# Memory attention in a two-block transformer kernel: GpSimd takes the low parts of the output projection's weights, and two orders of work change

## The reference, cut to what matters

```python
def _memory_cross_attention(h, mem, norm_mem_kv, w_q_mem, w_kv_mem, w_o_mem):
    B, S, _ = h.shape                                    # 1, 256, 1024
    q = (h @ w_q_mem).reshape(B, S, MEM_HEADS, MEM_HEAD_DIM)      # 4 heads of 128
    kv = _rmsnorm(mem, norm_mem_kv) @ w_kv_mem
    k, v = jnp.split(kv, 2, axis=-1)
    ...
    logits = jnp.einsum('bshd,bmhd->bhsm', q, k).astype(jnp.float32) * MEM_HEAD_DIM ** -0.5
    p = jax.nn.softmax(logits, axis=-1).astype(v.dtype)
    o = jnp.einsum('bhsm,bmhd->bshd', p, v).reshape(B, S, MEM_WIDTH)
    return o @ w_o_mem

        # in first_block:
        x = x + _rmsnorm(_memory_cross_attention(h, mem, ...), norm_mem_post)
        h = _rmsnorm(x, norm_ffn_pre)
        x = x + _rmsnorm(_swiglu(h, w_gate_up, w_down), norm_ffn_post)
```

## Time and profile before

| | |
|---|---|
| median of 3 runs | 1464.11 us (1464.03 to 1464.86) |
| the profiled execution's own time | 1464.0 us |
| its span, first to last instruction | 1462.2 us |
| busy share of the span: TensorE, VectorE, ScalarE, GpSimd | 99%, 74%, 47%, 14% |
| mean granted TensorE clock | 0.998 of full speed |
| the memory attention's heads and output projection | 218 to 246 us of the span |
| the norm, to the second block's transposes | 246 to 255 us |

### The profile page before, as it was taken

The page is one execution under the profiler, slowest core; times in us unless marked ns, Lnnn a source line. Parts: engine busy times, 40 slices in busy tenths (PEclk is TensorE's granted clock), DMA queues, the critical chain, the costliest instruction groups (busy, mean ns, idle before and its releaser), DMA issues.

```text
span 1462.2 us, 20856 instructions
## 1 busy us (share of the span) xinstructions
PE 1443.1 (99%) x7488; PEld 1219.0 (83%) x7488; DVE 1088.5 (74%) x1825; ACT 688.2 (47%) x854; POOL 207.4 (14%) x189
## 2 busy tenths in 40 slices
PE   9999999999999999999999999999999999999997
PEld 8988897888888888889988888888888897788886
DVE  5665767888778877757758877777887777688876
ACT  5346556444444444454435443465444377444442
POOL 1073011200001000300032000301000335510001
PEclk9999999999999999999999999999999999999999
DMA  8754653855656556566567566576556450475561
GB/s 275 243 173 142 198 174 124 299 188 182 212 183 213 172 188 213 172 207 198 169 206 237 172 198 206 174 239 212 179 180 217 144 183 30 132 239 176 179 214 66
DMA packets 198876, 274.48 MB, mean 188 GB/s; under 512 B 9632, under 2 KB 158240, under 8 KB 198560
## 3 DMA queue, kind: packets, MB, share of 16 engines
q1 hardware_dynamic: 194304, 256.62, 53.2%
q0 software_dynamic: 4368, 16.78, 3.3%
q10 hardware_dynamic: 144, 0.26, 0.0%
HBM read 272.32 MB, written 1.31 MB: 187 GB/s over the span
## 4 chain that ended last, share of the span: by engine, by line
PE 89%; DVE 3%; POOL 3%; ACT 3%; issue 1%; DMA 0%; DVEq 0%; SPq 0%; ACTq 0%; POOLq 0%
PE ps L646 25%; PE ps L647 25%; PE ps L648 25%; PE ps L758 3%; PE ps L752 3%; PE ps L741 3%; PE ps L687 1%; ACT whi L1415 1%; POOL wlo L2764 1%; DVE wlo L1986 1%; PE ps L805 1%; PE ps L1126 0%; PE ps L1254 0%; DVE big L2588 0%; POOL big L2809 0%
## 5 line engine op out<-in xcount | busy, mean ns | idle before, releaser
L1986 DVE TENSOR_TENSOR wlo<-raw,whi 128x2048 fp32r<-128x2048 f32 (+1 forms) x224 | 509.4, 2291 | 168.4 <-ACT whi L1415 166.5
L1415 ACT CAST whi<-raw 128x2048 fp32r<-128x2048 f32 (+1 forms) x239 | 452.7, 1894 | 373.0 <-PE ps L648 327.8
L646 PE MATMUL ps<-whi,st_hi 128*128 128x512 f32 (+1 forms) x1064 | 414.8, 390 | 0.3 <-DVE wlo L1986 0.3
L648 PE MATMUL ps<-whi,st_lo 128*128 128x512 f32 (+1 forms) x1064 | 412.5, 388 | 0.0
L647 PE MATMUL ps<-wlo,st_hi 128*128 128x512 f32 (+1 forms) x1064 | 412.4, 388 | 0.0
L2400 DVE STREAM_TRANSPOSE hidT<-hidden 32x128 f32<-32x128 f32 x800 | 242.3, 303 | 12.3
L646 PEld LDWEIGHTS ps<-whi,st_hi 128*128 128x128 f32 (+1 forms) x1064 | 198.9, 187 | 41.6 <-DVE wlo L1986 0.6
L648 PEld LDWEIGHTS ps<-whi,st_lo 128*128 128x128 f32 (+1 forms) x1064 | 198.8, 187 | 41.0
L647 PEld LDWEIGHTS ps<-wlo,st_hi 128*128 128x128 f32 (+1 forms) x1064 | 198.9, 187 | 40.0
L646 PE MATMUL ps<-whi,hid_hi 128*128 128x512 f32 x400 | 156.2, 390 | 0.0
L648 PE MATMUL ps<-whi,hid_lo 128*128 128x512 f32 x400 | 155.7, 389 | 0.0
(11 more groups left out here) (261 smaller groups left out, 1430.0 us busy)
## 6 DMA issues: line engine op xcount, KB each, us to landing
raw<-in_ffn_w SPq DMA_DIRECT2D x264, 512.0 KB, 4.8
raw<-in_w_gate_up SPq DMA_DIRECT2D x44, 512.0 KB, 4.7
raw<-in_w_in SPq DMA_DIRECT2D x32, 512.0 KB, 5.1
raw<-in_sgu_w_in SPq DMA_DIRECT2D x32, 512.0 KB, 4.7
raw<-in_w_down SPq DMA_DIRECT2D x22, 512.0 KB, 5.1
raw<-in_sgu_w_out SPq DMA_DIRECT2D x16, 512.0 KB, 4.7
raw<-in_kv_w SPq DMA_DIRECT2D x12, 512.0 KB, 4.5
raw<-in_w_proj_attn SPq DMA_DIRECT2D x8, 512.0 KB, 4.5
```

What stands on the lines that cost most here:

```text
L646: pe.matmul(o, a[0], b[0], start=start, stop=False)
L648: return pe.matmul(o, a[1], b[0], start=False, stop=stop)
L1415: act.copy(whi[:, s, 0:n], raw[:, s, 0:n]).then_inc(whi_ready, 1)
L1986: dve.tensor_tensor(wlo[:, s, 0:n], raw[:, s, 0:n], whi[:, s, 0:n].bitcast(F32), ALU.subtract).then_inc(wlo_ready, 1)
```

## The change

GpSimd's set gets om0 and om1, and GpSimd's program splits both right behind the load of the gain of the FFN's norm, ahead of the roots of the output. VectorE's calls at these two places go. ScalarE casts om1 right behind om0, before the exponentials. In the norm, VectorE scales both halves of block 1 before it brings block 0's first transposed part out, then adds block 1's two halves to the residual, and only then brings out block 0's second part.

```diff
-        BY_POOL |= {first["ffn", n] + 3 for n in range(5)}
+        BY_POOL |= {first["ffn", n] + 3 for n in range(5)} | {first["om"], first["om"] + 1}
...
             queries_out_m(0)
             beside(first["qm"])
+            beside(first["qm"] + 1)
             exp_m(0)
             exp_m(1)
             queries_out_m(1)
             turned_m(0)
-            beside(first["qm"] + 1)
             turned_m(1)
...
-            beside(first["qm"])
             max_m(0)
             max_m(1)
...
             heads_low_m(0)
             heads_low_m(1)
-            beside(first["qm"] + 1)
             heads_low_m(2)
             heads_low_m(3)
...
             scale_rms("mem", "ymem", 1, 0)
-            st_out("ffn0", 0)
             scale_rms("mem", "ymem", 1, 1)
+            st_out("ffn0", 0, part=0)
             add_rms("mem", "ymem", 1)
+            st_out("ffn0", 0, part=1)
             split_half(last + 2, 1)
...
             load_row(gb[:, 1, :], A["norm_ffn_pre"], gb_loaded[1])
+            for k in range(2):
+                split(first["om"] + k)
             rms_root("ymem", 0)
```

## The result

The changed kernel takes **1470.99 us** in the median of 6 runs (1469.93 to 1472.05), the kernel before 1464.07 us in 6 runs measured beside it: a ratio of 1.0047, with a 95% interval of 1.0037 to 1.0056. It is slower by 6.9 us, near the upper end of the range given (1463.0 to 1471.4) and 1.8 us above the 1469.2 forecast. The profiled execution took 1471.12 us, against 1464.0 before.

What follows compares the result with a forecast made beforehand. TensorE, 99% busy, was taken to bound the kernel, so only its waits could move the time. 1464.0 + 3.85 (heads) + 0 (norm) + 1.3 (clock) = 1469.2 us, range 1463.0 to 1471.4.

Steps and rivals of the forecast that it cites:

- the forecast's own course: Main case: head 0's two scalings held by GpSimd's splits, then a lower clock; 1467.9 to 1470.6 us, chance 0.60.
- the hold: Heads: VectorE's scalings of head 0 wait for GpSimd's splits of om0 and om1; +3.85 us for the stage.
- the clock: TensorE behind its 4.7 us gap in the heads: clock may fall to half; +1.3 us, bounds 0 and 2.7.
- What GpSimd's splits cost: Prediction's section on the heads: what VectorE is held from during GpSimd's 4.64 us splits; +3.85 us.
- the operation that decides here: Heads: the one-operand scaling of the probabilities, said to be held by GpSimd's splits, making turn_m(0) 4.42 us late.
- rival 2: Heads: the two-column negatives of the maxima are held as well; +4.6 instead of +3.85, 1469.9 us, chance 0.12.
- GpSimd goes first: Head 0's second scaling: GpSimd's second split takes its turn first, even asking 0.03 us later; VectorE held until 229.55.
- The norm's order: Norm: block 1's additions moved ahead still wait for GpSimd's half split; 0 us, bounds -1.2 and 0.
- The gain of the cast's place: Heads: om1's cast no longer stands ahead of head 2's exponential; without a new wait, some 0.8 us earlier.
- 0.9 off the exponential of head 2, of which head 3 keeps 0.8: Heads: the moved cast lets head 2's exponential start 0.9 us earlier and head 3's 0.8.

Runs made afterwards that it cites:

- e4: The changed kernel with 18 extra matmuls (128x512, result overwritten) keeping TensorE busy in its wait ahead of turn_m(0); 1469.88 us over 4 runs.
- e5: The changed kernel with the negatives of the maxima taken one column at a time, two instructions instead of one; 1470.89 us over 4 runs.
- e11: The changed kernel with 9 extra matmuls instead of 18 in TensorE's wait ahead of turn_m(0); 1471.19 us over 4 runs.
- e1: The kernel before with the new order of the norm alone; 1464.81 us, ratio 1.0007.
- e3: The changed kernel with GpSimd's splits of om0 and om1 cut to 16 of 2048 columns, other low parts left out; 1464.17 us, ratio 1.0002.
- e10: The kernel of e6 with the new order of the norm; 1464.41 us, ratio 1.0000.
- e9: The kernel before with the new norm order and GpSimd's half split cut to 16 of 1024 columns, other low parts left out; 1463.77 us, ratio 0.9996.
- e8: The kernel before with only om1's cast moved ahead of the exponentials; 1463.51 us over 11 runs, ratio 0.9997.
- e6: The changed kernel with one-column negatives, the old norm order, and GpSimd's split of om1 moved behind all four heads' scalings; 1463.62 us, ratio 0.9998.
- e2: The changed kernel with the old order of the norm; 1471.21 us over 4 runs.

## Why the prediction was right, and where it wasn't

The direction, the range and the kind of mechanism (a hold by GpSimd's splits, then a low clock) held: 1469.2 forecast, 1463.0 to 1471.4 given, 1470.99 measured. That is above the 1467.9 to 1470.6 of the forecast's own course, as three terms came out too small: the hold by 0.9 us, the clock and the norm by 0.6 each. Step by step:

- **The hold** was read rightly from the earlier trace rows, and its price is there: forecast +3.85 us for the heads by the two scalings alone, +4.6 with the negatives held too, measured 4.78 (e4), of which 0.1 may be the clock's. **The step that failed** is in "What GpSimd's splits cost", where I called the scaling "the operation that decides here". The negatives came first and hid the scalings. That was rival 2, to which I gave 0.12 on the strength of the earlier trace rows, an operation of one column. The changed kernel and e5 show both sides: two columns are held, one is not. The row was of the same operation and still not the nearest in what counted. It is luck that this miss was cheap: with the negatives held, `turn_m(0)` comes 0.70 us later than in e5 and the heads take 0.4 us more, because either course ends with GpSimd's second split. The Trainium skill ("VectorE: DVE Perf Modes", section "Mode 2×_2P — use both read ports for one tensor") counts float32 `tensor_scalar` from SBUF to SBUF among the operations that use both ports. The trace agrees down to two numbers per partition: 2.62 and 4.01 us instead of 0.17.
- **GpSimd goes first** at the second scaling came out in e5: 1.26 and 4.60 us where 1.3 and 4.6 stood in the text. That it does so even when it asks later, which was taken from 0.03 us in the earlier trace rows, e5 doesn't test: there GpSimd's split starts 0.04 us ahead.
- **The clock** fell, as the earlier trace rows suggested. The term was 1.3 us, the middle of 0 and 2.7; e4 puts it at 1.93 and e11, where the fall came later, at 1.6. The size was off, by 0.6.
- **The norm's order** was taken at 0, with bounds -1.2 and 0, and cost 0.6 (18.66 against 18.05 in e1; e3 and e10 have the same). That step was wrong, and outside its bounds. I had made sure that the later work fits ahead of `pre_norm`, for which VectorE "waits 0.92 us anyway", and had not asked what it does to the engine that VectorE waits for. The later half split holds GpSimd's root. Even the row that showed it was in the trace of before: that root took 0.45 us against 0.30 for the first ones, held a little by the same split. The gain without any hold was sized at up to 1.2; e9 has 0.7, because the root is held there too (1.04 us).
- **The gain of the cast's place** was sized at 0.8 and measured 0.54 in e3, 0.53 in e8. The step "0.9 off the exponential of head 2, of which head 3 keeps 0.8" failed at head 3: its exponential waits 0.28 us for its own negative in both, and starts 0.5 us earlier, not 0.8.
- Sum by the runs: 4.78 + 1.93 + 0.6 = 7.3 us against 1471.12 - 1464.0 = 7.1 in the profiled executions. The 4.78 is already net of the cast's gain. 0.2 us is less than what executions of one kernel differ by.

## What to carry to other kernels

Before work goes to GpSimd because it is idle, list what VectorE does in the stretch where GpSimd will be busy, and which of it works from SBUF to SBUF: here the scalings of 128x256, the negatives of 128x2 and the two-operand additions ended no sooner than GpSimd's split, while 128x1 and the reciprocals did not wait. GpSimd's long instructions belong beside VectorE's work on PSUM, as e6 has them. And when an order is changed so that VectorE "has the time anyway", look at what its instruction then stands beside: a 1.2 us split put 0.6 us on a root of one column. Last, a stall of TensorE can have a second price behind it: the 5.28 us of this one cost 4.78 us by themselves and 1.93 us, 40% of that, by the clock.

## What the runs showed of the hardware

- A `tensor_scalar` of VectorE on 128x2 numbers in SBUF, 0.17 us alone, took 2.62 and 4.01 us beside GpSimd's split; on 128x1 it took 0.15 (e5). The maxima, which read PSUM (0.68 and 0.69 us), and in e5 the reciprocal of 128x2 (0.17 us) were not held inside these splits.
- The hold works both ways: GpSimd's `tensor_scalar` of 128x1 took 1.05 us beside VectorE's two-operand split, and ended 0.17 us behind it. The Trainium skill ("SBUF — State Buffer", section "SBUF: two separate sides") has the port pair as an exclusive lock kept for a whole instruction. Beside GpSimd's splits and VectorE's the trace agrees in both directions.
- It does not agree beside every instruction of GpSimd: in the kernel before, VectorE's split at 1205.87 took its usual 2.29 us, although a scaling of GpSimd's (`tensor_scalar`, 128x256) is shown from 1205.29 to 1206.21.
- TensorE's clock fell to 1.2 GHz in or behind waits of 5.28 us (changed kernel, e2), 4.58 us (e5) and 3.28 us (e11), and stayed at 2.4 GHz where the wait was 1.30 us (e4). It was at half for 3.4 us in e11's profile and about 6.8 us in that of the changed kernel.
- A wait is not the only thing that came before such a fall. The profiled execution of e3 has one for 3.4 us from about 1219 us, in the second attention, and TensorE's timeline shows no wait ahead of it (from 1215.66 on it runs 32 matmuls of 64x16, then eight of 128x128). The kernel before has none there (clock 1.00 in its window). The window of e3:

```profile
1218.00:1222.00 4.00, 3.95 (x19) 2.73 (x16) 1.58 (x6) 1.65 (x4) 0.00 (x0) 0.61 0.00 0
```

This execution took 1465.97 us where e3's median is 1464.17. So part of the spread between runs may be this; it was not tested.
